# AdaLN projections of a hybrid diffusion backbone step: 40 of 48 units computed two or four at a time in shared PSUM rows, 24 of them loaded into buffers of their own

## The reference, cut to what matters

```
def ada_mods(cvec, w_ada, b_ada):
    m = jax.nn.silu(cvec) @ w_ada + b_ada
    return jnp.split(m[:, None, :], 6, axis=-1)
```

## Time and profile before

| what | value |
|---|---|
| median of 3 runs | 1049.16 us (1047.77 to 1050.31) |
| span of the profiled execution | 1047.8 us |
| PE busy, PE weight load busy | 97%, 90% |
| DVE, ACT, POOL busy | 54%, 46%, 13% |
| chain that ended last | PE 92%; DVE 3%; ACT 2% |
| read from HBM | 156.09 MB |

### The profile page before, as it was taken

How to read it: one execution, slowest core, us unless ns; L and a number is a source line. 1 busy time by engine, 2 the same in 40 slices (tenths; PEclk the granted TensorE clock), 3 DMA queues, 4 the chain that set the end, 5 groups by cost and what they waited for, 6 DMA issues and landing times.

```text
span 1047.8 us, 17863 instructions
## 1 busy us (share of the span) xinstructions
PE 1020.6 (97%) x7330; PEld 941.7 (90%) x7330; DVE 568.5 (54%) x914; ACT 486.1 (46%) x858; POOL 140.8 (13%) x173
## 2 busy tenths in 40 slices
PE   6999999999999999999999999999999999999997
PEld 3888885778999999999997989886999999999997
DVE  5556676564744345354457576576465445345452
ACT  5544665664553342342344556667464234252342
POOL 0162200011010010110110342350001011010110
PEclk9999999999999999999999999998999999999999
DMA  9987719645435445445445532223223524333311
GB/s 330 343 283 244 237 48 322 202 162 195 152 121 167 155 161 161 161 159 162 153 129 186 176 104 68 86 87 101 80 81 121 162 92 149 120 120 120 121 41 61
DMA packets 156974, 160.44 MB, mean 153 GB/s; under 512 B 3146, under 2 KB 155108, under 8 KB 156900
## 3 DMA queue, kind: packets, MB, share of 16 engines
q1 hardware_dynamic: 154512, 156.15, 45.0%
q0 software_dynamic: 704, 1.97, 0.6%
q10 hardware_dynamic: 1684, 1.26, 0.4%
HBM read 156.09 MB, written 3.28 MB: 152 GB/s over the span
## 4 chain that ended last, share of the span: by engine, by line
PE 92%; DVE 3%; ACT 2%; issue 1%; DMA 1%; SPq 0%; DVEq 0%; ACTq 0%
PE G L585 63%; PE G L590 13%; PE OB L607 4%; PE TB L554 4%; PE SC L918 2%; PE OB L932 1%; PE SC L694 1%; DMA raw<-in_w_ada 1%; PE OB L715 1%; PE OB L785 1%; PE TB L900 1%; ACT wH L1024 1%; PE SC L670 1%; PE SC L664 1%; PE SC L626 1%
## 5 line engine op out<-in xcount | busy, mean ns | idle before, releaser
L585 PE MATMUL G<-opH,wH 128*128 128x386 f32 (+1 forms) x768 | 267.7, 349 | 1.1 <-DVE wL L1505 0.8
L1024 ACT ACTIVATE wH<-raw 128x2048 fp32r<-128x2048 f32 x94 | 179.6, 1911 | 180.9 <-PE G L585 178.1
L585 PE MATMUL G<-opH,wL 128*128 128x386 f32 (+1 forms) x768 | 260.4, 339 | 0.0
L585 PE MATMUL G<-opL,wH 128*128 128x386 f32 (+1 forms) x768 | 260.2, 339 | 0.0
L1505 DVE TENSOR_TENSOR wL<-raw,wH 128x2048 fp32r<-128x2048 f32 x94 | 215.8, 2296 | 42.9 <-ACT wH L1024 42.9
L585 PE MATMUL G<-hidH,wH 128*128 128x384 f32 x512 | 173.3, 338 | 0.0
L585 PE MATMUL G<-hidH,wL 128*128 128x384 f32 x512 | 172.1, 336 | 0.0
L585 PE MATMUL G<-hidL,wH 128*128 128x384 f32 x512 | 172.1, 336 | 0.0
L585 PEld LDWEIGHTS G<-opH,wH 128*128 128x128 f32 x768 | 144.9, 189 | 9.8 <-issue 5.4
L585 PEld LDWEIGHTS G<-opL,wH 128*128 128x128 f32 x768 | 144.8, 189 | 1.6
L585 PEld LDWEIGHTS G<-opH,wL 128*128 128x128 f32 x768 | 144.9, 189 | 0.0
(11 more groups left out here) (246 smaller groups left out, 1192.6 us busy)
## 6 DMA issues: line engine op xcount, KB each, us to landing
raw<-in_w_mlp SPq DMA_DIRECT2D x64, 1024.0 KB, 5.2
raw<-in_w_ada SPq DMA_DIRECT2D x48, 1024.0 KB, 7.0
raw<-in_w_in_even SPq DMA_DIRECT2D x13, 1024.0 KB, 7.2
raw<-in_w_in_odd SPq DMA_DIRECT2D x12, 1024.0 KB, 5.1
raw<-in_w_out_even SPq DMA_DIRECT2D x4, 1024.0 KB, 6.6
raw<-in_w_out_odd SPq DMA_DIRECT2D x4, 1024.0 KB, 5.0
xin<-in_x_sample SPq DMA_DIRECT2D x2, 512.0 KB, 5.7
out_y_sample<-yout SPq DMA_DIRECT2D x1, 768.0 KB, 4.1
```

What stands on the lines that cost most here:

```text
L585: mm = pe.matmul(G[:, s, 512 * m:512 * m + cols], w[:, s, k, P * m:P * m + P], a[:, k, 0:cols], start=first and q == 0, stop=last and q == 2)
L1024: act.activation(wH[:, u % 2, :, :], raw[:, pos % RAW, :, :], ACT.Copy).then_inc(w_high, 1)
```

## The change

Units `a` 8 to 19 become six pairs, 20 to 47 become seven fours. Of a pair or four, unit b uses the stationary columns `cst[:, k, 6-2b : 38-2b]`, so that its two rows land in rows 2b and 2b+1 of each strip and the rest adds zeros; all matmuls accumulate into the same rows of `OB`. One copy, one turn and one reduction then serve the group. No matmul of an `ada_mm` goes away.

The fours are loaded by four 1 MB DMAs into a new buffer `adaw` that shares memory with the even mixers' tiles, and they leave the ring; the pairs stay in it.

```
+EVEN_PAIRS = [8, 10, 12, 14, 16, 18]
+QUADS = [20, 24, 28, 32, 36, 40, 44]
+QUAD_UNIT = {19: 20, 23: 24, 27: 28, 31: 32, 35: 36, 39: 40}
+QUAD_LOAD = {19: 20, 25: 24, 29: 28, 33: 32, 37: 36, 41: 40, 45: 44}
-MLP_ADAS = {20: 36, 23: 37, 26: 38, 29: 39, 32: 40, 35: 41, 38: 42, 41: 43}
-ODD_ADAS = {2: [44, 45, 46, 47]}
...
-                        sp.wait_ge(ob_full, OB_USE[f"ada{n}"] + 1)
+                        sp.wait_ge(ob_full, OB_USE[f"ada{pair_of(n)}"] + 1)
...
+            def load_quad(a):
+                if a == QUADS[0]:
+                    sp.wait_ge(gemm_done, 14)
+                    sp.wait_ge(out_dma, 16 * 3)
+                else:
+                    sp.wait_ge(ob_full, OB_USE[f"ada{a - 4}"] + 1)
+                for n in range(4):
+                    sp.dma_start(adaw[:, n, :, :], unit_cols(t["w_ada"][(a + n) // ADA_COLS], ((a + n) % ADA_COLS) * UC)
+                                 ).then_inc(adaw_in, 16)
...
+                for b in range(width):
+                    if width == 4:
+                        pe.wait_ge(adaw_in, 16 * (4 * QUADS.index(a) + 4))
+                        w = adaw[:, b, :, :]
...
+                    for k in range(KT):
+                        j = k % 4
+                        mm = pe.matmul(OB[32 * j:32 * j + 32, 0:UC], cst[:, k, 6 - 2 * b:38 - 2 * b], w[:, k, :],
+                                       start=b == 0 and k < 4, stop=b == width - 1 and k >= 4, skip_group_check=True,
+                                       tile_position=(0, 32 * j))
...
+                        if u == U_MLP0 + 4:
+                            dve.wait_ge(mods_set, ADA_ORDER.index(20) + 1)
```

More of the change, by code:

```diff
@@ L121 @@
 EVEN_PE = """
[L122 to L131, removed]
+    u2.03 u2.44 ada8 u2.56 adt8 u2.77 u3.04 u3.56 ada10 tq0 u3.77 adt10 u4.00 tq1 u4.11 tk u4.25 u4.66 ada12 sc0 u4.77
@@ new lines @@
+    u5.01 adt12 sc1 u5.23 u5.45 u5.67 u6.01 ada14 tpa0 u6.25 hg0 adt14 u6.67 hg2 u7.00 tpb0 sc2 u7.11 ada16 u7.23
+    adt16 pv0 hg4 tpa1 u7.47 hg6 u8.01 u8.22 hg8 ada18 tpb1 sc3 u8.33 adt18 u8.47 hg10 pv1 tpa2 u9.01 tpb2 sc4 pv2
+    tpa3 u9.23 tpb3 u9.44 sc5 u9.56 pv3 tpa4 u9.77 hg12 u10.04 hg14 tpb4 u10.55 u10.67 hg1 sc6 pv4 hg3 tpa5 tpb5 sc7
+    pv5 tpa6 tpb6 sc8 pv6 u11.01 hg5 u11.22 u11.33 tile0 turned0 u11.44 hg7 u11.56 u11.77 hg9 hgO0 tpa7 tpb7 sc9 pv7
+    u12.00 tpa8 hg11 u12.11 tpb8 sc10 pv8 tpa9 u12.22 hgO1 tpb9 sc11 u12.34 pv9 u12.55 tpa10 hg13 tpb10 state0 u12.67
@@ L143 @@
 """.split()
 EVEN_DVE = """
[L147 to L150, removed]
@@ L151 @@
-    adt31 grow9 ev10 mx9 adt26 share9 hg11 grow11 mx10 share10 sp13 mx11 adt27 share11 hg13 grow13 adt32 hg15 adt28
-    ins1 grow15 sp14 adt29 swo0 swo1 swo2 hgN0 swo3 gate0 hgH0 hgN1 gate1 hgH1 hgN2 gate2 hgH2 hgN3 gate3 adt33 hgH3
-    adt34 adt35
+    sp2.0 ev0 sp2.1 sp3 rs0 ev1 rs1 adt8 sp4 ev2 rs2 adt10 sp5 ev3 masks mx0 adt12 sp6 share0 mx1 ev4 share1 ev5 hf0
+    ks0 sp7 hg0 adt14 hg2 grow2 ev6 mx2 share2 adt16 hg4 grow4 sp8 hg6 grow6 ev7 hg8 grow8 mx3 adt18 sp9 share3 hg10
+    grow10 ev8 mx4 hf1 share4 mx5 sp10 hg12 grow12 share5 ev9 hg14 grow14 ins0 ks1 hg1 mx6 share6 hg3 grow3 mx7 sp11
@@ L154 @@
+    share7 mx8 share8 hg5 grow5 hg7 grow7 sp12 hg9 grow9 ev10 mx9 share9 hg11 grow11 mx10 share10 sp13 mx11 share11
+    hg13 grow13 hg15 ins1 grow15 sp14 swo0 swo1 swo2 hgN0 swo3 gate0 hgH0 hgN1 gate1 hgH1 hgN2 gate2 hgH2 hgN3 gate3
+    hgH3
 """.split()
-ADA_LATER = [a for u in range(13) for a in adas_of(u)] + list(range(34, 48))
 N_DIFF = 3 * H_C
 ODD_PE = """
[L163 to L170, removed]
@@ new lines @@
+    ns5 kc0 ns6 ada44 kc1 u0.00 adt44 u0.16 u0.77 u1.07 u2.03 tt0 u2.44 tt1 u2.57 u3.04 tt2 u3.55 tt3 d0 u3.67 d1 dP0
+    u4.02 tt4 u4.34 d2 tt5 u4.57 u5.00 d3 PV0 dP1 u5.12 PV1 dP2 d4 u5.33 tt6 PV2 u5.44 d5 u5.55 dP3 u5.67 PV3 dP4 d6
+    u6.03 d7 tt7 PV4 u6.44 dP5 u6.56 d8 PV5 dP6 u6.77 u7.01 d9 u7.25 tt10 d10 u7.66 tt11 u7.77 u8.00 d11 dN0 u8.12 PV6
+    tt12 u8.33 dN1 u8.45 tt13 u8.66 dP7 u8.77 PV7 dP8 u9.01 PV8 d12 dP9 u9.24 PV9 dP10 d13 u9.55 PV10 dN2 u9.67 d14
+    tt16 u10.01 tt17 u10.22 d15 dP11 u10.34 PV11 dP12 d16 u10.55 dN3 u10.67 tt18 u11.00 d17 PV12 dP13 u11.12 PV13 dP14
@@ L177 @@
[L177 to L180, removed]
+    sp1 sq lam kc0 nr sh0 sh1 kc1 ada44 sh2 sh3 sh4 sh5 sh6 sh7 ev0 sp2 rs0 ev1 sp3 rs1 tt0 tt1 ev2 sp4 rs2 tt2 tt3
@@ L231, in psum_uses @@
     sc.append("norm1")
-    for a in MLP_ADAS.values():
+    for a in QUAD_UNIT.values():
         ob.append(f"ada{a}")
@@ L376, in step_backbone_kernel @@
         shifts = small[:, 120:128].rearrange("p (s m c) -> p s m c", s=2, m=2)
-        adat = small[:, 96:100].rearrange("p (i c) -> p i c", c=2)
+        adat = small[:, 16:32].rearrange("p (i r) -> p i r", i=2)
         spans_of = [F[:, :, :, :],
@@ L517, in _ @@
             for pos in range(POS["u", U_MLP0], POS["u", U_ODD]):
[L518 to L522, removed]
+                n = STREAM[pos][1]
+                load(mlp_unit(0, (n - U_MLP0) % 8, (n - U_MLP0) // 8), pos)
+                if n in QUAD_LOAD:
+                    load_quad(QUAD_LOAD[n])
             for pos in range(POS["u", U_ODD], POS["u", U_MLP1]):
[L524 to L527, removed]
+                n = STREAM[pos][1]
+                if n < U_OUT_O:
                     load(unit_cols(t["w_in_odd"][0], ODD_COLS[n - U_ODD]), pos)
@@ L600, in ada_mm @@
             def ada_mm(a):
-                pos = POS["a", a]
-                pe.wait_ge(raw_in[pos % RAW], 16 * (pos // RAW + 1))
+                width = ada_width(a)
                 take("ob", f"ada{a}")
-                for k in range(KT):
-                    j = k % 4
-                    mm = pe.matmul(OB[32 * j:32 * j + 32, 0:UC], cst[:, k, :], raw[:, pos % RAW, k, :],
-                                   start=k < 4, stop=k >= 4, skip_group_check=True, tile_position=(0, 32 * j))
+                for b in range(width):
+                    if width == 4:
+                        pe.wait_ge(adaw_in, 16 * (4 * QUADS.index(a) + 4))
+                        w = adaw[:, b, :, :]
+                    else:
+                        pos = POS["a", a + b]
+                        pe.wait_ge(raw_in[pos % RAW], 16 * (pos // RAW + 1))
+                        w = raw[:, pos % RAW, :, :]
+                    for k in range(KT):
[3 more added lines that the diff above has]
+                                       tile_position=(0, 32 * j))
                 mm.then_inc(ob_full, 1)
@@ L1515, in ada @@
             def ada(a):
-                layer, j = a // ADA_COLS, 2 * (a % ADA_COLS)
+                layer, j, width = a // ADA_COLS, 2 * (a % ADA_COLS), ada_width(a)
                 full("tb", f"ada{a}")
-                n = ADA_FIRST.index(a) if a < 8 else ADA_LATER.index(a) + 8
+                n = ADA_ORDER.index(a)
                 if n:
                     dve.wait_ge(mods_set, n)
-                src = TB[:, 0:UC].rearrange("p (i g c) -> p i c g", i=2, g=4)[:, :, 0:2, :]
-                dve.tensor_reduce(adat, src, AX.X, ALU.add).then_inc(tb_free, 1)
+                src = TB[:, 0:UC].rearrange("p (i g r) -> p i r g", i=2, g=4)[:, :, 0:2 * width, :]
+                dve.tensor_reduce(adat[:, :, 0:2 * width], src, AX.X, ALU.add).then_inc(tb_free, 1)
                 dve.wait_ge(tb_free, TB_USE[f"ada{a}"] + 1)
-                b = bada[:, layer, j:j + 2].rearrange("p (i o) -> p i o", o=1).broadcast_to([P, 2, 2])
-                dve.tensor_tensor(mods[:, layer, j:j + 2, :], adat, b, ALU.add).then_inc(mods_set, 1)
+                for b in range(width):
+                    bias = bada[:, layer, j + 2 * b:j + 2 * b + 2].rearrange("p (i o) -> p i o", o=1).broadcast_to([P, 2, 2])
+                    ins = dve.tensor_tensor(mods[:, layer, j + 2 * b:j + 2 * b + 2, :], adat[:, :, 2 * b:2 * b + 2], bias,
+                                            ALU.add)
+                ins.then_inc(mods_set, 1)
             def scales(n, n_mods):
```

77 lines of the change are left out of this document (44 added, 33 removed).

## The result

After the change the kernel takes 1056.19 us (median of 9 runs, 1054.06 to 1058.93); beside it the kernel before takes 1049.16 us. The ratio is 1.0069, 95% interval 1.0056 to 1.0083: slower, where the prediction had 1045.6 us and faster. The profiled execution has a span of 1055.4 us against 1047.8: 7.6 us more, where the medians differ by 7.0.

What follows compares the result with a forecast made beforehand. The prediction took the kernel as PE-bound, except where mixer bursts may fill PE's waits. It summed -3.1 + 13.0 - 13.7 + 0.2 = -3.6 us, so 1049.16 became 1045.6 us, range 1040.5 to 1050.5.

Steps and rivals of the forecast that it cites:

- even mixers: Even mixers without units 20 to 35, sixteen bursts: -13.7 us of 19.5 to 22.4; bounds -19.5 and -6.3.
- Pairs, 8 to 19: Before 130 us, six bursts of two replace twelve singles, each saving 0.52 us: -3.1 us; bounds -3.6 to -1.5.
- joiner: A unit that joins another's burst: 0.88 us instead of 1.4 for its own burst; bounds 0.80 to 1.00.
- Fours in the first MLP: First MLP: six bursts with 24 units replace eight single bursts, +13.0 us; +11.6 to +15.2 by the bounds.
- walk: Job-by-job estimate of the even mixers' gain through four stretches, 154.9 to 258.1 us: sum -13.7 us.
- keeps one: Mixers: the sum keeps one stretch at 0.50 of the clock, costing some 1.5 us.
- Odd norm: DVE's alternation of nbuf and opL holds PE, so three bursts less gain nothing: +0.2 us, bounds -0.6 and +1.2.
- the third (clock): Mixers: two or more further stretches at 0.50 of the clock, 1048.6 us, no change; chance 0.13.
- The second rival: DVE-ACT loop holds the mixers, bursts were filler through most of 154.9 to 230.4 us: sum +3.1, 1052.3 us; chance 0.09.
- Rival 1: Mixers give back everything, -19.5 instead of -13.7: -9.4, 1039.8 us; chance 0.15.
- 4 (loads late): Loads of fours late in the first MLP or for unit 20: 2 to 8 us back, 1047.6 to 1053; chance 0.04.

Runs made afterwards that it cites:

- run 10: Kernel before with only units 8 to 19 as six pairs, and cst of 40 columns: 1046.68 us, ratio 0.9973.
- run 2: Kernel after with cst of 40 columns instead of 38, moving all behind it 64 bytes further: 1052.76 us, ratio 1.0028 to before.
- run 11: Kernel after with cst of 40 columns and four unread matmul fillers on PE, ahead of hg1, hg3, tpb6 and tile1: 1047.55 us, ratio 0.9986 to before.
- runs 1: Kernel before with cst of 38 columns instead of 32, moving all behind it 192 bytes further: 1053.44 us, ratio 1.0056.
- run 9: Kernel before with only the hidden operand's arena moved, by 192 unread bytes; one profiled execution: hidden units 8.48 us in both MLPs.
- run 7: Kernel after with cst of 40 columns, units 20 to 35 singly in the even mixers, fours only for 36 to 47: 1042.91 us, ratio 0.9942 to before.
- run 6: Kernel before with opH and opL rows of 392 columns instead of 386: 1051.38 us, ratio 1.0034.

## Why the prediction was wrong

The profiled span grew by 7.6 us where 3.6 less was forecast, 11.2 off (10.6 by the medians). Two terms failed: the even mixers, -13.7 forecast and -8.3 measured, and the layout, which the sum took at nothing and which cost 5.1. Step by step:

- **Pairs, 8 to 19**: -3.1 forecast, -2.1 measured (unit 9's end; 2.2 over all profiles, run 10). The joiner was priced rightly: a pair is 1.86 us in the chain of after, two singles 2.00 and a second turn and restart. What was missed is that PE arrives earlier at work of others. Chain of after behind the burst of 10 and 11:
```profile
66.33 1.64 POOL qout L2060
...
68.03 1.95 POOL qout L2063 x4
...
70.03 0.87 PE SC L574 x6
```
The turn of Q waits there for POOL until 69.98, some 0.5 us that the second burst seems to have covered: in before no POOL work stands in the chain there. I had argued from PE being 100% busy in the stretch; that says that PE never waited before, not that nothing stands close behind. The rest is not traced.
- **Fours in the first MLP**: +13.0 forecast; +12.6 in run 2, where the layout is cured. No DMA of the extra loads stands in the chain, as forecast. Right.
- **Even mixers**: -13.7 forecast, -8.3 measured. This is the step of the walk that failed, in two parts. At full clock on both sides the gain is 11.7 (runs 10 and 11; at least that, since run 11 carries the fillers), so the walk was 2.0 too good: up to unit 11 it gave 5.0 and 4.5 came (14.0 + 30.8 against 11.5 + 28.8), from there to unit 13 it gave 8.7 and 7.2 came, where I walked less closely. Of the 2.4 at `sc8`, 0.65 was the burst of 24, which ran at half clock in before: in runs 10 and 11 `sc8` comes 1.7 sooner, no more than wH. That was a gain of clock, counted as work. The other 3.4 us are clock. I wrote that the sum "keeps one" stretch at 0.50; after has 13.7 us at 0.50 in one piece and a further 3.5 us at 222.3, and the mixers of after take 5.0 us more than with fillers, those of before 1.6 more than in run 10.
- **Odd norm**: +0.2 forecast; unit 48's to unit 49's end takes 0.2 less. From unit 48's end to the first `opL` it was 7.3 us before (562.85 to 570.18) and is 6.9 now.
- **Not in the sum at all**: the layout, +5.1 us, 32 hidden units at 8.48 instead of 8.32 (runs 1, 2 and 9; the two MLP windows of after are 2.5 us longer than run 2's and 2.4 longer than before's). The diff shows it in one line, `cst` of 38 columns, and I didn't ask what lies behind it. It is nearly half of the miss.

1.0 + 2.0 + 3.4 + 5.1 - 0.4 - 0.4 = 10.7 of the 11.2. The rest, 0.5, lies in one gap between GEMM matmuls that no edit touched, from 716.9 to 728.2 us in before and from 721.3 to 733.2 in after, 11.3 and 11.9 us long. The clock falls to 0.50 in both, from 720.6 and from 727.5 us, and in run 9, where it stays full, the gap is 9.6 us; what makes the 0.5 isn't shown.

Of the rivals, the third (clock) named the right mechanism and was too small: two stretches and +3.0. That rule, that gaps between matmuls cost the clock ("TensorE: Matmul & The Clock Gate" in the Trainium skill, section "Why this matters for your kernels"), was set against a row in which it had happened once, and the row won. The trace of after and run 11 agree with the direction of the rule; the page speaks of longer gaps than the 2.09 and 1.98 us behind which the clock fell here, and the measurement decides. The row came from a kernel whose gaps were filled by the very bursts that the change removes, so it couldn't tell what happens without them. The second rival (the loop through `SC`) had about the right size, an even gain of 7 where 8.3 came, but by luck and for the wrong reason: in run 11 the loop is as it was and the gain is 11.7. Rival 1 (everything back) and 4 (loads late) fell.

What the change does by itself, without layout and lost clock but with four fillers, is run 11: 1047.55 us, 1.2 us under before (0.3 to 2.6 by the interval). It is no more because moving units 20 to 35 out of the mixers is a loss even then: their fours make the first MLP 16.1 us longer (286.4 us in run 11, 270.3 in run 7), and the mixers give back 11.7.

## What to carry to other kernels

Where another engine sets the pace, filler on PE isn't waste, as taking it out can give back far less than its own time. Here six bursts between the ends of units 10 and 11 gave nothing, as the clock fell, and 2.0 us with the clock kept (30.8 against 28.8). Count how long PE will stand idle after the change, not only what it idled before. Batching small bursts pays in a stretch of PE work alone (0.4 us for each burst that joins another ahead of the mixers, some 0.55 in the first MLP, where run 7 has six joiners and is 3.4 us shorter than before) and should stop where the mixers start: run 7, which batches at both ends and leaves the middle, is 0.6% faster than before, where batching all was 0.7% slower, 0.3% without the layout (run 2). And a tensor that grows moves all behind it: compare the pace of the unchanged loops first, a difference there was layout here.

## What the hardware showed that was not expected

- The place of the moving operand in SBUF changes the pace of a matmul of 384 columns. `hidH` 192 bytes further: 1320 matmuls in 233.83 us instead of 231.79 (of which half stream `hidH` or `hidL`; 8.48 instead of 8.32 us for a unit's 48). 32 and 256 bytes further it was as fast as before. No rule came out of it: with 384 bytes further (run 6) one MLP was fast and the other slow, so that the address of this operand alone doesn't decide.
- The granted clock fell to 0.50, 1.2 instead of 2.4 GHz, behind waits of PE of 2.09 and 1.98 us (after, 164.3 to 178.0 us) and did not where the same gaps were filled with matmuls that no one reads (run 11). Here are the 8.6 us ahead of that point, in after and then in run 11; PE is busy 4.04 and 7.85 us:
```profile
155.70:164.30 8.60, 4.04 (x119) 2.48 (x117) 4.98 (x14) 2.75 (x10) 0.85 (x2) 1.00 0.01 2
156.90:165.50 8.60, 7.85 (x152) 6.36 (x150) 4.97 (x13) 2.75 (x9) 1.00 (x2) 1.00 0.01 2
```
- Near 720 us, where no kernel of the study differs, the clock fell in nearly all profiles, for 3.4 to 6.8 us, but not in that of run 9; so single profiles differ by a few us through it.
- Profiles of the same code differ by some 2 us ahead of unit 9 (its end is at 144.4 us in run 10 and 146.5 in run 7, whose PE work is the same up to there). A term of 1 or 2 us is read from differences between ends of units, not from the span.
